# One run of dense slices per turn of the sliding attention, and the low part of a weight block in four GpSimd pieces

## The reference

```python
def window_gqa_sink(h, w_qkv, w_out, sink):
    qkv = h @ w_qkv
    ...
    o, lse = banded_attention(q, k, v, slopes, 1, WINDOW_A, BLOCK_A)
    o = o * jax.nn.sigmoid(lse - sink...)[..., None]
    return o.astype(h.dtype).reshape(b, s, H_A * HEAD_DIM) @ w_out

def first_block(x, ...):
    for i in range(DEPTH):
        h = rmsnorm(x, norm_mix[i])
        x = x + (window_gqa_sink(...) if i % 2 == 0 else dilated_mixture_attention(...))
        h = rmsnorm(x, norm_ffn[i])
        x = x + swiglu(h, w_gate[i], w_up[i], w_down[i])
    return rmsnorm(x, norm_final)
```

## Time and profile before

| | us |
|---|---|
| median of 3 runs | 2172.48 (2170.53 to 2172.78) |
| the profiled execution, its own time | 2174.57 |
| its span in the profile | 2173.2 |
| sliding attention, scores of the first unit to the last value products | 34.3 to 158.8 |
| TensorE busy | 2145.1 |
| VectorE, ScalarE, GpSimd busy | 997.2, 799.3, 734.5 |

### The profile page before, as it was taken

How to read it: one execution, slowest core, us unless ns; L and a number is a source line. 1 busy time by engine, 2 the same in 40 slices (tenths; PEclk the granted TensorE clock), 3 DMA queues, 4 the chain that set the end, 5 groups by cost and what they waited for, 6 DMA issues and landing times.

```text
span 2173.2 us, 30673 instructions
## 1 busy us (share of the span) xinstructions
PE 2145.1 (99%) x12586; PEld 1754.2 (81%) x12586; DVE 997.2 (46%) x1764; ACT 799.3 (37%) x1371; POOL 734.5 (34%) x339
## 2 busy tenths in 40 slices
PE   9999999999999999999999999999999999999999
PEld 8778888888889898888878888887886667886677
DVE  5664555541222333334465555345305673552672
ACT  6445333333333333334443333333225442334531
POOL 3116444455443333333174444443221002232102
PEclk9999999999999999999999999999999999999999
DMA  4103444432322222221034444322110001322002
GB/s 153 40 30 110 145 145 146 144 126 97 107 93 88 82 81 82 78 88 69 35 121 146 145 146 146 135 97 95 59 68 35 1 1 40 110 78 83 1 2 78
DMA packets 57659, 191.53 MB, mean 88 GB/s; under 512 B 8112, under 2 KB 11440, under 8 KB 57264
## 3 DMA queue, kind: packets, MB, share of 16 engines
q1 hardware_dynamic: 46128, 155.82, 20.6%
q10 hardware_dynamic: 11392, 33.75, 4.4%
HBM read 185.35 MB, written 2.10 MB: 86 GB/s over the span
## 4 chain that ended last, share of the span: by engine, by line
PE 88%; DVE 3%; ACT 1%; issue 1%; DVEq 1%; POOL 0%; ACTq 0%; POOLq 0%; DMA 0%
PE ps L180 21%; PE ps L181 21%; PE ps L182 21%; PE ps L2729 4%; PE ps L183 3%; PE ps L185 3%; PE ps L184 3%; PE ps L2761 2%; PE ps L2741 2%; PE ps L1105 2%; PE ps L1139 1%; PE ps L1121 1%; PE ps L2284 0%; PE ps L2250 0%; PE ps L2097 0%
## 5 line engine op out<-in xcount | busy, mean ns | idle before, releaser
L253 POOL TENSOR_TENSOR w_lo<-w_raw,w_hi 128x1024 fp32r<-128x1024 f32 x282 | 682.0, 2419 | 1332.2 <-ACT w_hi L170 1318.0
L170 ACT ACTIVATE w_hi<-w_raw 128x1024 fp32r<-128x1024 f32 x284 | 300.3, 1058 | 539.3 <-DMA w_raw<-in_wstream 539.0
L180 PE MATMUL ps<-h_hi,w_hi 128*128 128x512 f32 x1168 | 464.0, 397 | 2.7 <-DVE w_lo L295 1.8
L182 PE MATMUL ps<-h_hi,w_lo 128*128 128x512 f32 x1168 | 455.0, 390 | 0.0
L181 PE MATMUL ps<-h_lo,w_hi 128*128 128x512 f32 x1168 | 455.0, 390 | 0.0
L180 PEld LDWEIGHTS ps<-h_hi,w_hi 128*128 128x128 f32 x1168 | 219.3, 188 | 50.7 <-DVE w_lo L295 2.0
L182 PEld LDWEIGHTS ps<-h_hi,w_lo 128*128 128x128 f32 x1168 | 219.3, 188 | 46.0
L181 PEld LDWEIGHTS ps<-h_lo,w_hi 128*128 128x128 f32 x1168 | 219.5, 188 | 43.3 <-issue 0.7
L183 PE MATMUL ps<-w_hi,h_hi 128*128 128x256 f32 x416 | 116.6, 280 | 0.0
L185 PE MATMUL ps<-w_hi,h_lo 128*128 128x256 f32 x416 | 115.5, 278 | 0.0
L184 PE MATMUL ps<-w_lo,h_hi 128*128 128x256 f32 x416 | 115.5, 278 | 0.0
(11 more groups left out here) (362 smaller groups left out, 4019.5 us busy)
## 6 DMA issues: line engine op xcount, KB each, us to landing
w_raw<-in_wstream SPq DMA_DIRECT2D x283, 512.0 KB, 3.2
f0mod_rows<-in_wmod ACTq DMA_DIRECT2D x24, 512.0 KB, 4.6
f1mod_rows<-in_wmod ACTq DMA_DIRECT2D x24, 512.0 KB, 4.6
dvS<-dvE SPq DMA_DIRECT2D x64, 32.0 KB, 2.5
out<-x SPq DMA_DIRECT2D x8, 256.0 KB, 3.2
x<-in_x SPq DMA_DIRECT2D x3, 512.0 KB, 6.9
l_dft<-in_dft ACTq DMA_DIRECT2D x4, 384.0 KB, 4.2
l_wuq<-in_wuq ACTq DMA_DIRECT2D x2, 768.0 KB, 6.1
```

The costliest lines, as they stand in the source:

```text
L170: self.A.activation(self.slot(self.w_hi, n), self.slot(self.w_raw, n), ACT.Copy).then_inc(self.w_high, 1)
L180: T.matmul(out, wh, ah, start=start, stop=False)
L182: return T.matmul(out, wl, ah, start=False, stop=stop)
L253: G.tensor_tensor(c.slot(c.w_lo, n), c.slot(c.w_raw, n), c.slot(c.w_hi, n).bitcast(F32), ALU.subtract).then_inc(c.w_low, 1)
```

## The change

Three edits. First, in a turn of the sliding attention the two portions of slices become one, which stands after the value products, at the end of the turn; the order is scores, transposes, value products, slices. Second, `DONE` runs a little ahead: eight slices in three turns up to turn 14 instead of five in two up to turn 15, so that 16, 40, 48, 56 and 64 slices are done one turn earlier, and the pieces of the out projection begin in turn 27, one in each turn. Third, GpSimd makes a block's low part by four instructions of 256 columns; only the last one raises `w_low`.

```diff
+QUARTER = 256
...
         G.wait_ge(c.w_high, n + 1)
-        G.tensor_tensor(c.slot(c.w_lo, n), c.slot(c.w_raw, n), c.slot(c.w_hi, n).bitcast(F32),
-                        ALU.subtract).then_inc(c.w_low, 1)
+        for a in range(0, 1024, QUARTER):
+            b = a + QUARTER
+            low = G.tensor_tensor(c.slot(c.w_lo, n)[:, a:b], c.slot(c.w_raw, n)[:, a:b],
+                                  c.slot(c.w_hi, n)[:, a:b].bitcast(F32), ALU.subtract)
+        low.then_inc(c.w_low, 1)
...
-    DONE = [min(64, (5 * (u + 1) + 1) // 2 if u < 16 else 40 + 2 * (u - 15)) for u in range(UNITS)]
+    DONE = [min(64, (8 * (u + 1) + 2) // 3 if u < 15 else 40 + 2 * (u - 14)) for u in range(UNITS)]
...
             goal = self.DONE[u] if u < self.UNITS else 64
-            half = (done + goal) // 2
             if u == 0:
-                self.slices(0, half)
+                self.slices(0, 2)
+                done = 2
             if u < self.UNITS:
                 self.scores(u)
             if u % 4 == 1 and u > 4:
                 self.spread_out_of(u // 4 - 1)
-            if u:
-                self.slices(done, half)
             if 1 <= u <= self.UNITS:
                 self.turn_probs(u - 1)
-            self.slices(half, goal)
-            if u == 28:
+            if 2 <= u <= self.UNITS:
+                self.sum_values(u - 2)
+            self.slices(done, goal)
+            if u == 27:
                 T.wait_ge(self.evacuated, 10)
                 T.wait_ge(self.spread_out, 6)
-            if u >= 28:
-                out.pieces(2 if u == 28 else 1)
-            if u >= 2:
+            if u >= 27:
+                out.pieces(1)
+            if u > self.UNITS:
                 self.sum_values(u - 2)
             done = goal
```

## The result

The changed kernel takes 2177.83 us (median of 7 runs, 2175.76 to 2180.64), the kernel before 2172.58 in the same session (7 runs): a ratio of 1.0027, 95% interval 1.0015 to 1.0038, that is 5.2 us more, with 3.3 and 8.3 as the ends. The profiled execution took 2180.04, its span is 2178.7.

What follows compares the result with a forecast made beforehand. TensorE, busy 99% of the span, was taken as the bound; sliding attention +3.3 and the out projection's fifth block +0.9 make +4.2 us on 2172.48: 2176.7 us, range 2171.0 to 2180.5 (forecast's own 2174.5 to 2178.5).

Steps and rivals of the forecast that it cites:

- The price of the new order: Sliding attention: four changes of array shape a turn instead of three, +0.14 us in turns 2 to 26, +4.4 us together.
- Rival A: Sliding attention: the change from transposes to value products is free, giving 2171.4 us or less; chance 15%.
- The sliding attention as a whole: Turns cost 4.4 us more, shorter waits for query tiles give back 1.1: +3.3 us.
- I found no wait of TensorE for an operation of VectorE that itself stood behind a low part: Whole kernel: VectorE getting on sooner thanks to the four pieces was priced at nothing.
- Otherwise I count no new wait: Sliding attention: apart from the kept 0.86 us wait for `wRD`, the new order adds no TensorE wait.
- rival C: Sliding attention, tile copies in turns 14, 18, 22, 26 delay ScalarE: four waits of 0.68 us, 2179.4 us; chance 12%.
- The fifth block of the out projection: Second out projection: four pieces +0.35 and a VectorE operation between them +0.55, so +0.9 us, a wait of 2.9.
- Rival B: Fifth block: VectorE comes in at every border, +2.2 us, and the lower clock may add 1.7: 2179.7 us; chance 16%.
- A loss of some 1.7 us that I leave as it is: Behind the fifth block's wait: the lower clock for 3.4 us costs some 1.7 us, taken as unchanged.

Runs made afterwards that it cites:

- e3: The changed kernel with the joined slices between transposes and value products instead of behind the value products: 2172.80 us, 1.0002 of before.
- e2: The kernel before with only the low parts made in four pieces: 2174.96 us, 1.0009 of before.
- e1: The changed kernel with each low part in one instruction again, the new order kept: 2178.30 us, 1.0025 of before.
- e5: The changed kernel with the joined slices between transposes and value products and each low part in one instruction: 2172.49 us, 1.0000 of before.
- e9: e3 with the second out projection's fifth block in one instruction and 16 products into an unread bank ahead of its wait: 2173.10 us, 1.0000 of before.
- e4: The kernel before with the new `DONE` alone, low parts in one instruction: 2175.04 us, 1.0007 of before.
- e7: The changed kernel with 16 products into an unread PSUM bank ahead of the wait for the fifth block: 2177.77 us, 1.0025 of before.

## Why the prediction was right, step by step

**The price of the new order: right, and to its size.** Transposes that come behind scores and go on to value products were put at 0.78 and take 0.80; turn 11 was put at 3.83 and takes 3.84. The comparison of e3 and the changed kernel makes 0.17 a turn of the very pair that no row of before showed, and that is the 31 x 0.17 = 5.3 that the prediction gave as its bound. Rival A falls. The Trainium skill, "TensorEngine Tiling (Array Packing)", section "Tiling Modes", says that a change of mode drains TensorE; 0.80 against 0.62 agrees. That the change of shape makes the whole 0.17 is not shown. The reciprocals take 0.49 ahead of transposes and 0.41 ahead of a slice, and there no shape changes: some of a group's price can lie in what follows it, shape or not, and no run here parts the two.

**The sliding attention as a whole: nearly right in the sum, with two terms left out that cancel.** The prediction has +3.3; measured is +3.8 in both pairs of profiles. Added up by groups, transposes cost 6.6 in place of 6.0, the reciprocals 0.5 that wasn't forecast (0.08 more ahead of transposes than ahead of a slice, six times) and a wait in turn 28 0.3; against that, slices give back 2.7 in place of 2.1 and value products 1.1 in place of 0.8. The larger miss doesn't show in the sum: the step "I found no wait of TensorE for an operation of VectorE that itself stood behind a low part, so that VectorE gets on sooner is priced at nothing". It was read from a trace of the old order, for which e2 confirms it (125.06). In the new order it is wrong: without the pieces three waits for the reciprocals stand there, 2.0 us (e1). The step "Otherwise I count no new wait" is wrong in the same place: the new DONE brings low parts beside the small sums. What the one edit adds the other takes away, so a prediction that left out both came out right; here it was lucky. Of rival C's four waits for the probabilities one is there, 0.24 in turn 28; what threatens in the others is VectorE held up by GpSimd, not ScalarE's copy, and the pieces keep it from TensorE.

**The fifth block of the out projection: right.** The wait was put at 2.9, and is 3.04 and 2.92; the pieces were put at 2.75 + 0.55 = 3.30 with VectorE's operation between them and last 3.28. Rival B would have VectorE come in at every border; one operation did.

**The clock behind that wait: an assumption that one profile can't carry.** "A loss of some 1.7 us that I leave as it is" was 2.8 in one execution of the changed kernel, 1.4 in another, and nothing in e3. No run shows that the difference belongs to the change: e2, with as long a wait, has the same stretch behind it as before. The two first spans are 5.5 us apart, the second ones, 2175.6 and 2172.7, only 2.9, since the changed kernel has the longer stretch at the lower clock in the first pair and one stretch fewer than before in the second.

**What stays open.** Stage and wait make 3.8 + 0.9 to 1.0, that is 4.7 to 4.8 us by the profiles, where 4.2 was predicted. The medians say 5.2, with 3.3 to 8.3: they agree, and don't settle the last half microsecond. Between medians e2 is 2.4 above before where the rows show 1.1, and e3 is level with e5 although its sliding attention is 1.4 shorter; both lie within the intervals. A cost spread over the 1128 pieces would have to show in the 891.6 us between the two stages or behind the out projection, and there profiles with and without pieces agree to 0.1 us. What is left is how often the clock falls in one kernel and in the other, and these runs, with one or two profiles each, don't tell.

## What to carry to other kernels

A group of products has a price that depends on its neighbours, so cost a new order by pairs (what stands before, what behind), and look for the pair in other stages of the same trace where the stage in question lacks it. When an edit moves the moment at which a helper engine works, list what the other engines do at that new moment; a "no wait there" read from the old order isn't evidence for the new one. Try the parts of a change apart even where the sum fits: here one part alone gains (joined slices, -2.5 us), one loses 5 us (the slices behind the value products), and two hide each other (the new `DONE` and the pieces). Before filling a wait, check how long the filling itself lasts: in e9 it outlasted the wait by 0.8 us.

## What the runs showed of the hardware that was not expected

- A VectorE addition of 128x8 elements with two inputs in SBUF, 0.16 us alone, took 2.10, 0.99 and 0.44 us beside GpSimd instructions of 1024, 512 and 256 columns (0.76 in e3, where it began just past a border). Splitting the GpSimd instruction lets VectorE in at the next border: VectorE is busy 37 us less, GpSimd 207 more, 0.73 a block on average over the 282 blocks.
- Behind a wait of the same length the granted clock may fall to 0.5 (1.2 GHz) or not: 2.9 us with none (e3), 2.92 with some 2.9 us of it and 3.04 with 5.6 us (the changed kernel), 2.1 with none (e4), 2.0 with some 3 us (the kernel before). It stayed at 1.00 in both kernels with products in the gap (e7, e9); as e3 and e4 show the same without, two profiles don't make that a remedy.
- A gain on TensorE of 2 us or less was partly taken back 28 us later by GpSimd's sums of rows (0.5 to 0.9 in e3, e7 and e9), an engine that is busy 43% of the span in the changed kernel. With whole low parts (e4) it was not.
- Four transposes of 128x128 take 0.41 us ahead of a slice and 0.49 ahead of further transposes, in the same use of the array (128\*128): what follows a group has a price even without a change of shape.
